# Convolution drain of a fused transformer kernel: the taps spread over four half slots, the second sigmoid and both products one chunk later, PSUM banks waited for one by one

## What is computed

```python
    qa, ka, va, zb, xbc, dtb, qc, kc, vc, gpre = jnp.split(h @ w_in, SPLIT_POINTS, axis=-1)
    ...
    xbc = lax.conv_general_dilated(            # causal, depthwise, 4 taps
        xbc, conv_w[:, None, :], window_strides=(1,), padding=[(CONV_B - 1, 0)],
        dimension_numbers=('NWC', 'WIO', 'NWC'), feature_group_count=CONV_DIM) + conv_b
    xbc = jax.nn.silu(xbc).astype(jnp.float32)
    xs, bm, cm = jnp.split(xbc, [D_INNER, D_INNER + G_B * N_B], axis=-1)
```

## Time and profile before

| what | value |
|---|---|
| median of 3 runs (lowest, highest) | 2024.05 us (2023.79, 2024.33) |
| time of the profiled execution | 2023.97 us |
| span of its profile | 2022.2 us |
| TensorE busy with matmuls | 2000.3 us, 99% of the span |
| VectorE, ScalarE busy | 1397.8 us, 1097.2 us |
| mean granted TensorE clock | 0.999 |

### The profile page before, as it was taken

How to read it: one execution, slowest core, us unless ns; L and a number is a source line. 1 busy time by engine, 2 the same in 40 slices (tenths; PEclk the granted TensorE clock), 3 DMA queues, 4 the chain that set the end, 5 groups by cost and what they waited for, 6 DMA issues and landing times.

```text
span 2022.2 us, 35322 instructions
## 1 busy us (share of the span) xinstructions
PE 2000.3 (99%) x14178; PEld 1824.1 (90%) x14178; DVE 1397.8 (69%) x2098; ACT 1097.2 (54%) x1761; POOL 147.5 (7%) x150
## 2 busy tenths in 40 slices
PE   8999999999999999999999999999999999999998
PEld 7889899899988889998999989998888989899996
DVE  7877788745556686778775656656678677886555
ACT  6677466534444577658544443434558756753442
POOL 1200000000000001710000000000000370000000
PEclk9999999999999999999999999999999999999999
DMA  7434556535745544643645744575453554464563
GB/s 281 163 126 131 176 187 228 188 130 187 253 164 167 167 134 149 199 157 133 220 138 187 249 167 159 186 251 179 144 168 126 166 190 146 147 208 147 187 209 124
DMA packets 272892, 354.71 MB, mean 175 GB/s; under 512 B 10212, under 2 KB 226046, under 8 KB 272766
## 3 DMA queue, kind: packets, MB, share of 16 engines
q1 hardware_dynamic: 271421, 348.71, 51.3%
q0 software_dynamic: 1344, 4.23, 0.7%
HBM read 351.83 MB, written 1.08 MB: 175 GB/s over the span
## 4 chain that ended last, share of the span: by engine, by line
PE 88%; DVE 5%; ACT 3%; issue 1%; DMA 1%; POOL 1%; SPq 0%; DVEq 0%; ACTq 0%
PE ps L808 25%; PE ps L810 17%; PE ps L817 17%; PE ps L818 7%; PE ps L812 7%; PE ps L802 3%; PE ps L804 3%; PE ps L803 3%; DVE ring_r L1963 1%; DMA ring<-in_w_in 1%; PE ps L1328 1%; POOL small L2737 1%; PE ps L1259 1%; ACT ring_hi L1453 1%; PE ps L1051 1%
## 5 line engine op out<-in xcount | busy, mean ns | idle before, releaser
L1963 DVE TENSOR_TENSOR ring_r<-ring,ring_hi 128x1024 fp32r<-128x1024 f32 x602 | 733.4, 1225 | 409.8 <-ACT ring_hi L1453 408.0
L1453 ACT ACTIVATE ring_hi<-ring 128x1024 fp32r<-128x1024 f32 x602 | 632.4, 1059 | 595.3 <-PE ps L817 377.6
L808 PE MATMUL ps<-xT_hi,ring_hi 128*128 128x256 f32 x2784 | 680.7, 284 | 0.8 <-DVE xT_r L1963 0.8
L810 PE MATMUL ps<-xT_r,ring_hi 128*128 128x256 f32 x2784 | 670.7, 280 | 0.0
L808 PEld LDWEIGHTS ps<-xT_hi,ring_hi 128*128 128x128 f32 x2784 | 523.5, 188 | 16.0 <-issue 11.2
L810 PEld LDWEIGHTS ps<-xT_r,ring_hi 128*128 128x128 f32 x2784 | 524.0, 188 | 0.1
L817 PE MATMUL ps<-xT_hi,ring_r 128*128 128x256 f32 x2784 | 384.0, 280 | 0.0
L817 PEld LDWEIGHTS ps<-xT_hi,ring_r 128*128 128x128 f32 x2784 | 352.1, 188 | 0.0
L2737 POOL TENSOR_TENSOR small<-small,const 128x1 f32<-128x1 f32 (+3 forms) x32 | 39.7, 1241 | 1832.2 <-DVE small L2412 1265.4
L812 PE MATMUL ps<-ring_hi,tok_r 128*128 128x512 f32 x344 | 135.7, 395 | 0.0
L808 PE MATMUL ps<-ring_hi,xT_hi 128*128 128x512 f32 x328 | 131.9, 402 | 1.4 <-issue 0.9
(11 more groups left out here) (380 smaller groups left out, 2865.0 us busy)
## 6 DMA issues: line engine op xcount, KB each, us to landing
ring<-in_w_mix_in SPq DMA_DIRECT2D x88, 1024.0 KB, 5.0
ring<-in_ffn_w_in SPq DMA_DIRECT2D x80, 1024.0 KB, 5.0
ring<-in_ffn_w_out SPq DMA_DIRECT2D x44, 1024.0 KB, 4.8
ring<-in_w_branch SPq DMA_DIRECT2D x24, 1024.0 KB, 5.1
ring<-in_w_ffn_up SPq DMA_DIRECT2D x22, 1024.0 KB, 5.0
ring<-in_w_in SPq DMA_DIRECT2D x21, 1024.0 KB, 5.0
ring<-in_w_ffn_down SPq DMA_DIRECT2D x11, 1024.0 KB, 4.8
ring<-in_w_mix_out SPq DMA_DIRECT2D x8, 1024.0 KB, 5.5
```

What stands on the lines that cost most here:

```text
L808: pe.matmul(out_, stat[0], mov[0], start=first, stop=False)
L810: pe.matmul(out_, stat[0], mov[1], start=False, stop=False)
L1453: act.activation(half_of(high_of(s), s, q), half_of(ring[:, s % SLOTS, :], s, q), ACT.Copy).then_inc(w_hi, 1)
L1963: return dve.tensor_tensor(lo, whole, hi.bitcast(F32), ALU.subtract)
```

## The change

Three things. The drain of an xbc chunk gets a new shape: ScalarE's four activations are done two in part 0 and two in part 1, VectorE's six taps of a bank three in each of two parts (bank 0 in parts 0 and 1, bank 1 in parts 2 and 3), and the sigmoid of bank 0 in part 2. The sigmoid of bank 1 and the product of bank 0 become a step `conv_first`, behind part 0 of the drain of the next chunk, and the product of bank 1 a step `conv_second`, behind its part 1. And TensorE waits for a chunk's two banks one by one: the second one ahead of the first product that writes it.

```diff
+    for i, c in enumerate(mix):
+        if c.name == "xbc":
+            steps.insert(steps.index(("drain", mix[i + 1], 0)) + 1, ("conv_first", c))
+            steps.insert(steps.index(("drain", mix[i + 1], 1)) + 1, ("conv_second", c))
...
-    before(("drain", [c for c in mix if c.name == "xbc"][2], 3), ("turn_xs", 0))
+    before(("conv_second", [c for c in mix if c.name == "xbc"][2]), ("turn_xs", 0))
...
+            def wait_free_bank(c, b):
+
+                if c.need[b]:
+                    pe.wait_ge(drained[b], c.need[b])
...
-                if h == 0 and q == 0:
-                    wait_free(c)
+                if (h, q) == (0, 0):
+                    wait_free_bank(c, 2 * c.pair)
+                    if c.event is not None:
+                        wait_free_bank(c, 2 * c.pair + 1)
+                elif (h, q) == (1, 0) and c.mode == "B":
+                    wait_free_bank(c, 2 * c.pair + 1)
...
                     for t, k in places:
+                        if (t, h, k) == (1, 0, 0):
+                            wait_free_bank(c, 2 * c.pair + 1)
                         mov = [v[:, k, :] for v in w]
...
-                    elif c.name == "xbc" and part == 0:
-
-                        wait_products(act, L, c)
-                        if c.index:
-                            act.wait_ge(xbc_done, lap(L, 2 * c.index, 6))
-                        for j in range(2):
-                            for f in range(2):
...
-                            ins_.then_inc(xbc_begun, 1)
-                    elif c.name == "xbc" and part < 3:
...
+                    elif c.name == "xbc" and part < 2:
+
+                        if part == 0:
+                            wait_products(act, L, c)
+                            if c.index:
+                                act.wait_ge(xbc_done, lap(L, 2 * c.index, 6))
+                        for f in range(2):
...
+                        ins_.then_inc(xbc_begun, 1)
+                    elif c.name == "xbc" and part == 2:
+                        conv_sigmoid(c, 0)
...
+                def conv_sigmoid(c, j):
+
+                    b = 2 * c.pair + j
+                    act.wait_ge(drained[b], c.need[b] + 1)
+                    chain.link(act.activation(act_s[:, j, :], conv_s[:, j, :], ACT.Exp, scale=-1.0))
+                    chain.sync()
+                    sigmoid([act_s[:, j, :]], xbc_exp)
+
+                def conv_first(c):
+                    conv_sigmoid(c, 1)
...
                     elif c.name == "xbc":
-                        j = part - 2
...
+
+                        j = part // 2
...
+                        if part % 2 == 0:
+                            dve.wait_ge(xbc_begun, lap(L, 2 * c.index + j + 1, 6))
+                            link(tap(1, 0))
+                            link(tap(1, 1))
+                            sync()
+                            link(tap(2, 0))
+                        else:
+                            sync()
+                            link(tap(2, 1))
+                            link(tap(3, 0))
+                            sync()
+                            tap(3, 1).then_inc(drained[2 * p + j], 1)
...
+                def conv_product(c, j):
+
+                    dve.wait_ge(xbc_exp, lap(L, 2 * c.index + j + 1, 6))
+                    k = 4 * c.index + 2 * j
+                    dve.tensor_tensor(xbc[:, k:k + 2, :], feats_of(act_s[:, j, :]), feats_of(conv_s[:, j, :]), ALU.mult).then_inc(xbc_done, 1)
+
+                def conv_first(c):
+                    conv_product(c, 0)
+
+                def conv_second(c):
+                    conv_product(c, 1)
```

More of the change, by code:

```diff
@@ L1757, in drain @@
                         sigmoid(places, z_exp)
-                    elif c.name == "xbc" and part == 0:
-                        wait_products(act, L, c)
-                        if c.index:
-                            act.wait_ge(xbc_done, lap(L, 2 * c.index, 6))
-                        for j in range(2):
-                            for f in range(2):
[L1765 to L1768, removed]
-                            ins_.then_inc(xbc_begun, 1)
-                    elif c.name == "xbc" and part < 3:
[L1772 to L1776, removed]
+                    elif c.name == "xbc" and part < 2:
[4 more added lines that the diff above has]
+                        for f in range(2):
+                            k = 4 * c.index + 2 * part + f
+                            ins_ = act.activation(conv_s[:, part, f * TOK:(f + 1) * TOK], tiles(2 * p + part)[:, f, :], ACT.Identity,
+                                                  scale=cols[:, P + 3 * N_XBC + k:P + 3 * N_XBC + k + 1],
+                                                  bias=cols[:, P + 4 * N_XBC + k:P + 4 * N_XBC + k + 1])
+                        ins_.then_inc(xbc_begun, 1)
+                    elif c.name == "xbc" and part == 2:
+                        conv_sigmoid(c, 0)
                     elif c.name in ("qc", "kc"):
@@ L1912, in kout @@
                     ins_.then_inc(s_copied, 1)
-                attention = dict(turn_qk=turn_qk, dscore=dscore, dturn=dturn, dout=dout, turn_oa=turn_oa,
+                attention = dict(conv_first=conv_first, turn_qk=turn_qk, dscore=dscore, dturn=dturn, dout=dout, turn_oa=turn_oa,
                                  sdecay=sdecay, ysquare=ysquare, snorm=snorm, bhigh=bhigh, kscore=kscore, ksoft=ksoft, ksum=ksum, kout=kout, drain=drain)
@@ L2474, in drain, with tap @@
                             dve.tensor_tensor(zT[:, k:k + 2, :], tiles(2 * p + j), feats_of(conv_s[:, j, :]), ALU.mult).then_inc(drained[2 * p + j], 1)
[L2475 to L2488, removed]
-                    elif c.name == "xbc":
-                        j = part - 2
-                        dve.wait_ge(xbc_exp, lap(L, 2 * c.index + j + 1, 6))
-                        k = 4 * c.index + 2 * j
-                        dve.tensor_tensor(xbc[:, k:k + 2, :], feats_of(act_s[:, j, :]), feats_of(conv_s[:, j, :]), ALU.mult).then_inc(xbc_done, 1)
+                    elif c.name == "xbc":
+                        j = part // 2
+                        def tap(shift, f):
+                            k = P + (3 - shift) * N_XBC + 4 * c.index + 2 * j + f
+                            o = conv_s[:, j, f * TOK + shift:(f + 1) * TOK]
+                            return dve.scalar_tensor_tensor(o, tiles(2 * p + j)[:, f, 0:TOK - shift], cols[:, k:k + 1], o, ALU.mult, ALU.add)
+                        if part % 2 == 0:
[10 more added lines that the diff above has]
+                            tap(3, 1).then_inc(drained[2 * p + j], 1)
                     elif c.name in ("qc", "kc"):
@@ L2697, in ksum @@
                     dve.tensor_tensor(own, own, ps[:, TB, :].rearrange("p (m b n) -> p m b n", m=2, n=P), ALU.subtract).then_inc(s_arg, 1)
-                attention = dict(turn_qk=turn_qk, dscore=dscore, dweigh=dweigh, dnorm=dnorm, cb=cb, turn_xs=turn_xs, sdecay=sdecay, sout=sout,
+                attention = dict(conv_first=conv_first, conv_second=conv_second, turn_qk=turn_qk, dscore=dscore, dweigh=dweigh, dnorm=dnorm, cb=cb, turn_xs=turn_xs, sdecay=sdecay, sout=sout,
                                  turn_oa=turn_oa, bsplit=bsplit, osplit=osplit, ysum=ysum, snorm=snorm, kscore=kscore, ksoft=ksoft, klow=klow, ksum=ksum, drain=drain)
```

## The result

The changed kernel takes 2029.05 us in the median of 18 runs (2027.02 to 2033.96), the kernel before 2024.49 in the median of 18 (2022.43 to 2026.23). The ratio is 1.0025, with a 95% interval of 1.0019 to 1.0032: slower by 4.6 us, a little over the 0.2% that a measurement can tell.

What follows compares the result with a forecast made beforehand. TensorE, busy 99%, was taken as the bound, so only its waits count. Per layer 2.4 + 0.3 - 0.95 = 1.75 us, 3.5 in all, gave 2027.6 us, 0.17% slower; range 2024.6 to 2030.6 us.

Steps and rivals of the forecast that it cites:

- Hold in va 7: After va 7's first four matmuls TensorE waits 3.1 us for its second bank; 2.4 us more than before per layer.
- The chain: From va 6's end through ScalarE's split, VectorE's split and three taps: bank freed at 698.00, TensorE resumes at 698.10 us.
- Hold in ka 4: Second bank released at 661.19 us but wanted at 660.90: 0.3 us lost per layer, where there was nothing.
- the cover: Row product between qa 3 and ka 4, delaying ka 4's start to 659.97 us and so hiding most of its wait.
- xbc 8: Spreading this drain removes two attention waits; gain between 0 and 1.3 us per layer, taken as 0.95.
- The mask's 0.5: At xbc 8, the mask comes about 1.4 us earlier on VectorE, so TensorE's 0.5 us wait goes.
- the old copy's 0.8: At xbc 8, ScalarE's copy L1839 runs some 2 us earlier with the second sigmoid moved, so 0.8 us go.
- the new late copy: One chunk after xbc 8, ScalarE's copy comes late behind the moved sigmoid, estimated at 0.35 us.
- The overdraft: ScalarE's quarter with moved sigmoid and two gate exponentials: 2.5 + 0.8 + 1.9 against 4.0 us, 1.2 too much.
- The clock, rival 3: Clock falls in each new hold, doubling the next half slot: 2 x 2.8 us more, 2033.2 us; 5%.
- Rival 2: In gate 10, copy L1839 misses TensorE's turn once or twice; xbc 8's gain becomes a loss, 2031.5 us; 14%.
- Rival 1: Hold does not come, VectorE reaching the last taps before TensorE wants the bank; 3.1 us gained, 2020.9 us; 10%.

Runs made afterwards that it cites:

- third set: Runs on a third chip, kernel before beside them at 2024.68 us; the changed kernel, unaltered, took 2032.64 us there, ratio 1.004.
- the last run: New drain for the third xbc chunk only, and on ScalarE its second sigmoid moved behind the split, against the kernel before: 2020.25 us, ratio 0.9978.

## Why the prediction was right, and where not

- **Forecast and range.** 2027.6 us was forecast, 2029.05 came, inside 2024.6 to 2030.6. By the chances, though, the likeliest class was no change that can be told (0.59), and it was slower (0.38). That the median fell so near is in part luck: without the low clock the change costs 4.05 us and not 3.5, and in the third set of runs the same kernel took 2032.64 us, above the range, by the clock that the sum had left out. The four fastest of the 18 runs, 2027.0 to 2027.3, are no measure of the change without the clock; the kernel before has such fast executions as well, its four fastest are 2022.4 to 2023.7, 4.1 lower. Nor is the clock the whole spread: one of the 18 runs, 2029.26 us, had a granted clock of 1.000.
- **Hold in va 7.** Forecast 3.1 us of delay and 2.9 idle, measured 3.00 and 2.83. The chain held link by link; that the new drain of xbc 5 causes it is shown by the run that keeps the old one.
- **Hold in ka 4.** Forecast 0.3, measured 0.3, and 3.0 without the row product: the cover was the right one.
- **xbc 8.** The gain was forecast as 0.95 us a layer. It was 1.30 - 0.66 = 0.64 in layer 0 and 1.30 - 0.48 = 0.82 in layer 1. The mask's 0.5 and the old copy's 0.8 went as said; the term that was mis-sized is the new late copy, put at 0.35 us. The overdraft was reckoned from busy times, but ScalarE stood idle for the peak ahead of it, so not all of its free time could be used. That the idle time was usable is shown by the run with the sigmoid in the gap. The losses add up to 2.4 (3.00 less the 0.60 of the old wait ahead of va 7), 0.3 at ka 4 and -0.73 at xbc 8 (the mean of the two layers), 1.97 us a layer, 3.9 in all, against 3.5 forecast. The run with TensorE kept busy puts it at 4.05.
- **The clock, rival 3.** The step that failed is "by the rows the pause is just short of it, and the sum stays without it". That rival had 5%, at 5.6 us more for two falls. In the profiled execution the clock fell behind both holds and cost 2.85 and 1.56 us there, 4.4 in all. Over all runs it is neither absent nor certain: the median lies 0.5 us above the price without it in the first 18 runs and 3.9 above it in the third set. The rows of the program's end showed one pause of 3 us at full clock, and I took that as a bound, where one case can't give one. That pause was even longer, TensorE's last matmul ends at 2015.2 us:

```profile
2015.20:2019.10 3.90, 0.00 (x0) 0.00 (x0) 3.79 (x9) 0.00 (x0) 0.99 (x1) 1.00 0.00 0
```

So 3.9 us without a matmul went by at full clock there, and holds of 2.4 and 2.8 us did not in part of the executions here: the length of the pause alone does not decide it in these runs. The Trainium skill (TensorE: Matmul & The Clock Gate, the part on the HAM clock gate) says that an array that stays idle long enough falls to half rate. The fall itself is in the runs, but behind pauses shorter than the one that page names; here the measurement decides.
- **Rival 2** was right in its place and far too high in its price: one new wait in gate 10, which cost 0.5 to 0.7 us and left more than half of the gain. The prediction named a new wait in gate 10, and a clock other than 0.999, as signs against it, and both are there: TensorE's busy time rose by 8 us and the mean clock of the profiled execution was 0.995.
- **Rival 1** falls: the bank came when the chain said, and the hold was there in both layers.

## What to carry to other kernels

When a drain is spread over more steps, ask for each buffer when its next user first wants it and not when the old drain freed it: here one and the same change gained behind a mode B user and lost 2.4 us behind a mode A user that wants the bank after 0.93 us. A wait moved to the last possible place is cheap and can be worth much more than it looks (20 us here, 2048.7 against 2029.1). Where an engine stands idle for another, put the moved work in just that gap, by its order on that engine alone; where a short stall of TensorE can't be avoided, independent matmuls in it can keep the clock full, as they did in both profiles here.

## What the runs showed that I had not expected

- The clock falls behind pauses of 2.4 and 2.8 us, in some executions and not in others of the same kernel. It also fell at 236 us in five of the twelve profiles, around waits of 1.1 and 0.8 us in the first block, which none of the kernels changes; the other seven, with the same waits, had it full there. What decides this is open.
- Between 236 and 356 us, in the first block's FFN, TensorE's pace differs by 1% between executions: the profiles of the kernel before, of the run with the cover removed and of the last run took 1.3 us less for it than the other nine. I have no cause for it, and it is more than a quarter of the difference that was to be measured here; it tells to compare medians of many runs and not two profiles.
